# One inference step of a hybrid trunk layer on one core: the samples' page loop, the mixer's sample part and the last down projection in another order

## What is computed

```python
# samples: 1024 past rows in 8 pages of 128, blocks of 32 rows compressed by a two-layer net
ck = rms_norm(compress_block(cmp_rows[:, :, :, 0], phi_k_w1, phi_k_w2), k_cmp_g)   # gelu between the layers
cv = compress_block(cmp_rows[:, :, :, 1], phi_v_w1, phi_v_w2)
s_s = einsum(q, k_selected) ; s_w = einsum(q, k_window)            # scores against the paged and the window keys
# recurrent mixer, one step for each sample and head (4 heads of 128)
S = exp(g)[..., None] * S + k v^T ; o = q S ; o = rms_norm(o, hg_norm_g) * silu(gate)
# feed-forward: 2816 hidden channels in 22 tiles of 128
x = x + (silu(conv(xn2 @ w_gate)) * (xn2 @ w_up)) @ w_down
```

## Time and profile before

| | |
|---|---|
| median of 3 runs | 2120.39 us (2115.72 to 2124.99) |
| the profiled execution | 2122.58 us |
| its span, first to last instruction | 2120.8 us |
| PE busy | 1991.6 us (94%) |
| DVE, ACT, POOL busy | 879.7, 588.8, 155.1 us |
| mean granted clock of PE | 0.953 of full |
| bytes moved by DMA | 148.17 MB |

### The profile page before, as it was taken

How to read it: one execution, slowest core, us unless ns; L and a number is a source line. 1 busy time by engine, 2 the same in 40 slices (tenths; PEclk the granted TensorE clock), 3 DMA queues, 4 the chain that set the end, 5 groups by cost and what they waited for, 6 DMA issues and landing times. The chain is left out here.

```text
span 2120.8 us, 38332 instructions
## 1 busy us (share of the span) xinstructions
PE 1991.6 (94%) x15620; PEld 1771.9 (84%) x15620; DVE 879.7 (41%) x1690; ACT 588.8 (28%) x1192; POOL 155.1 (7%) x214
## 2 busy tenths in 40 slices
PE   5889979999988699897999999999999999999997
PEld 4668656565664688887999999999999999999997
DVE  6223025565612267732223334544334424442453
ACT  5123136555512224413212222211112211111121
POOL 4000001000030033410000000000000000000000
PEclk8899959999999799978999999999999999999999
DMA  8421553000054511213222123111111111111112
GB/s 236 64 69 62 218 128 113 2 2 1 2 171 178 164 32 33 53 42 88 75 75 57 40 63 87 54 49 41 48 52 47 40 49 50 49 38 52 50 30 92
DMA packets 164842, 148.17 MB, mean 70 GB/s; under 512 B 7745, under 2 KB 152082, under 8 KB 163650
## 3 DMA queue, kind: packets, MB, share of 16 engines
q1 hardware_dynamic: 153636, 124.82, 19.7%
q0 software_dynamic: 6208, 17.67, 3.4%
q10 hardware_dynamic: 4864, 3.79, 0.7%
HBM read 120.54 MB, written 29.99 MB: 71 GB/s over the span
## 5 line engine op out<-in xcount | busy, mean ns | idle before, releaser
L247 PE MATMUL psum<-xgl,t_wh 128*128 128x344 f32 x1056 | 338.5, 321 | 0.0
L246 PE MATMUL psum<-xgh,t_wh 128*128 128x344 f32 x1056 | 338.3, 320 | 0.0
L248 PE MATMUL psum<-xgh,t_wl 128*128 128x344 f32 x1056 | 337.6, 320 | 0.0
L247 PEld LDWEIGHTS psum<-xgl,t_wh 128*128 128x128 f32 x1056 | 198.7, 188 | 0.1
L248 PEld LDWEIGHTS psum<-xgh,t_wl 128*128 128x128 f32 x1056 | 198.5, 188 | 0.0
L246 PEld LDWEIGHTS psum<-xgh,t_wh 128*128 128x128 f32 x1056 | 198.3, 188 | 0.1
L248 PE MATMUL psum<-hh,t_wl 128*128 128x344 f32 x528 | 169.2, 320 | 0.0
L246 PE MATMUL psum<-hh,t_wh 128*128 128x344 f32 x528 | 169.1, 320 | 0.0
L247 PE MATMUL psum<-hl,t_wh 128*128 128x344 f32 x528 | 169.0, 320 | 0.0
L466 ACT ACTIVATE t_wh<-t_raw 128x1024 fp32r<-128x1024 f32 x75 | 79.1, 1055 | 205.9 <-PE psum L248 205.9
L518 DVE TENSOR_TENSOR t_wl<-t_raw,t_wh 128x1024 fp32r<-128x1024 f32 x100 | 122.0, 1220 | 34.3 <-ACT t_wh L466 29.2
(11 more groups left out here) (430 smaller groups left out, 3867.9 us busy)
## 6 DMA issues: line engine op xcount, KB each, us to landing
t_raw<-in_w_gate SPq DMA_DIRECT2D x22, 512.0 KB, 3.8
t_raw<-in_w_up SPq DMA_DIRECT2D x22, 512.0 KB, 3.9
t_raw<-in_w_down SPq DMA_DIRECT2D x24, 384.0 KB, 3.4
cmp_pages<-in_cache_kv SPq DMA_DIRECT2D x64, 128.0 KB, 2.2
t_raw<-in_w_in SPq DMA_DIRECT2D x16, 512.0 KB, 4.2
raw_n<-in_w_in SPq DMA_DIRECT2D x24, 256.0 KB, 3.9
r_raw<-in_w_in SPq DMA_DIRECT2D x12, 512.0 KB, 4.4
xh_copy<-xh SPq DMA_DIRECT2D x1, 4128.0 KB, 12.7
```

Source lines behind the costliest of these rows:

```text
L246: pe.matmul(out, wh, xh, start=(first and k == 0), stop=False)
L247: pe.matmul(out, wh, xl, start=False, stop=False)
L248: mm = pe.matmul(out, wl, xh, start=False, stop=(last and k == n - 1))
```

## The change

It has three parts.

1. Page loop: all 128 compression steps come first. Then 24 turns of four transposes (3 for each sample) alternate between banks 7 and 3, and between ACT (even turns) and DVE (odd turns) as the engine that copies them out. The second product stands behind turn 2, the norm's product behind turn 6; scores stand behind every sixth turn as before. `t` and `sq` move to the place of `cmp_pages`, the window loads for samples 2 to 7 to SP's queue, and the reload of `xh` and `xl` now waits for the finished compressed keys.
2. Mixer: keys and values of the four heads lie in four groups of 32 rows, padded with zeros (`k8c`, `v8`). One transpose turns all keys; one POOL operation masks all values, in slot 10; two outer products for two heads each; in the read the queries (one column, repeated 32 times) are stationary and the state's 128 columns move, so each sample's result fills a quarter of 32 rows; ACT and DVE copy it out and two turns of four transposes bring it back to columns.
3. Tail: the last group's `w_down` is split into high and low parts once and kept (`dh`, `dl`), and its product runs over three ranges of columns (0 to 384, 768, 1032), all 8 channels in each. Between channels of the first range stand the transposes of the gate tail, between those of the second and third the transposes of x2 for the tokens of the range before; `store_y` is gone as a block.

Core of the diff, page loop:

```diff
+    bank = lambda q: 3 if q % 2 else 7
+
+    def evacuate(engine, op, q, done):
+
+        s, x = divmod(q, 3)
+        engine.wait_ge(S["tp"], q + 1)
+        if s >= 2:
+            engine.wait_ge(S["sc"], s // 2)
+        to = kwt[:, s % 2, :] if x == 2 else kst[:, s % 2, x * 512:(x + 1) * 512]
+        op(to, c.psum[:, bank(q), :]).then_inc(done, 1)
...
-            sp.wait_ge(S["p1"], 2)
+            for s in range(2, NS):
+                sp.wait_ge(S["tp"], 3 * (s - 2) + 3)
+                sp.dma_start(kwin[:, s % 2, :, :], kw_v[s, :, :, 0:P]).then_inc(w_in[s % 2], 16)
+            sp.wait_ge(S["ck"], 1)
             sp.dma_start(c.xh[:, :, :].bitcast(F32).rearrange("p k t -> p (k t)"), c.xh_dram).then_inc(S["xback"], 16)
             sp.dma_start(c.xl[:, :, :].bitcast(F32).rearrange("p k t -> p (k t)"), c.xl_dram).then_inc(S["xback"], 16)
...
+            def turn(q):
+                s, x = divmod(q, 3)
+                if x == 0:
+                    pe.wait_ge(sel_sp[s], 4 * 16)
+                    pe.wait_ge(sel_pool[s], 4 * 16)
+                if x == 2:
+                    pe.wait_ge(w_in[s % 2], 16 * (s // 2 + 1))
+                if q >= 2:
+                    pe.wait_ge(S["ev"] if q % 2 else S["ea"], q // 2)
+                if q == 1:
+                    pe.wait_ge(S["h"], 2)
                 for p in range(4):
-                    mm = pe.transpose(c.psum[:, TB, p * P:(p + 1) * P], sel[:, s * 8 + 4 * half + p, 0:P], c.ident[:, :])
+                    at = kwin[:, s % 2, p, :] if x == 2 else sel[:, s * 8 + 4 * x + p, 0:P]
+                    mm = pe.transpose(c.psum[:, bank(q), p * P:(p + 1) * P], at, c.ident[:, :])
                 mm.then_inc(S["tp"], 1)
 
...
             order = [(kv, d) for d in range(HD) for kv in range(2)]
-            compress(0, 80)
-            for s in range(NS):
-                x = 80 + 6 * s
-                turn(s, 0)
-                compress(x, x + 2)
-                turn(s, 1)
-                compress(x + 2, x + 4)
-                turn_window(s)
-                compress(x + 4, x + 6)
-                if s % 2:
-                    score(s - 1)
-            pe.wait_ge(S["h"], 2)
-            for g in range(GROUPS):
-                mm = pe.matmul(c.psum[g * HD:(g + 1) * HD, 0, 0:NB], c.w2[0:HD, 0, 0:HD], h[0:HD, g, :], start=True, stop=True)
-            mm.then_inc(S["p2"], 1)
...
+            compress(0, 2 * HD)
+            for q in range(3 * NS):
+                turn(q)
+                if q == 2:
+                    pe.wait_ge(S["h"], 2)
+                    for g in range(GROUPS):
+                        mm = pe.matmul(c.psum[g * HD:(g + 1) * HD, 0, 0:NB], c.w2[0:HD, 0, 0:HD], h[0:HD, g, :], start=True, stop=True)
+                    mm.then_inc(S["p2"], 1)
+                    for s in range(NS):
+                        for g in range(GROUPS):
+                            at = (s % 4) * P + g * HD
+                            mm = pe.matmul(c.psum[0:32, 1 + s // 4, at:at + HD], h[HD:P, g, s * 32:(s + 1) * 32], c.w2[HD:P, 1, HD:P],
+                                           start=True, stop=True)
+                    mm.then_inc(S["p2"], 1)
+                if q == 6:
+                    pe.wait_ge(S["sq"], 1)
+                    pe.matmul(c.psum[:, 0, NB:2 * NB], c.halves[:, :], sq[:, :], start=True, stop=True).then_inc(S["p3"], 1)
+                if q % 6 == 5:
+                    score(q // 3 - 1)
             for b in (5, 6):
                 pe.matmul(c.psum[:, b, :], c.tabrep[:, :], c.one_s[:, 0:512], start=False, stop=True)
```

Mixer (PE, then POOL):

```diff
+                pe.transpose(c.psum[:, X, 0:P], k8c[:, :, :].rearrange("p h s -> p (h s)"), c.ident[:, :]).then_inc(k8_t, 1)
+
+            def sample_outer(h0):
+                if h0 == 0:
+                    pe.wait_ge(k8_done, 1)
+                    pe.wait_ge(vm_done, 1)
                     pe.wait_ge(at_done, 7 * NH)
                     pe.wait_ge(coarse_done, NH)
-                if h >= 2:
-                    pe.wait_ge(new_state, NS * (h - 1))
+                else:
+                    pe.wait_ge(new_state, NS * h0)
                 for j in range(2):
-                    mm = pe.matmul(c.psum[:, X + 2 * ((h + 1) % 2) + j, :], k8[:, h * P:(h + 1) * P], vm[h % 2][:, j * 512:(j + 1) * 512],
-                                   start=True, stop=True)
-                mm.then_inc(outer, 1)
-
-            def sample_read(h):
-                pe.wait_ge(new_state, NS * (h + 1))
-                if h == 0:
+                    for h in (h0, h0 + 1):
+                        r32 = slice(32 * h, 32 * h + 32)
+                        mm = pe.matmul(c.psum[:, X + 2 * ((h + 1) % 2) + j, :], k8[r32, :], vm[r32, j * 512:(j + 1) * 512],
+                                       start=True, stop=True)
+                        if j:
+                            mm.then_inc(outer, 1)
+
+            def sample_read(h0):
+                pe.wait_ge(new_state, NS * (h0 + 2))
+                if h0 == 0:
                     pe.wait_ge(logged, NH)
-                for s in range(NS):
-                    mm = pe.matmul(c.psum[:, O, h * NS + s:h * NS + s + 1], ss[h][:, s * P:(s + 1) * P], q8[:, h, s:s + 1], start=True, stop=True)
+                for h in (h0, h0 + 1):
+                    for s in range(NS):
+                        g0 = 32 * (s % 4)
+                        at0 = (2 * (h % 2) + s // 4) * P
+                        mm = pe.matmul(c.psum[g0:g0 + 32, O + h0 // 2, at0:at0 + P], q8[:, h, s:s + 1].to_broadcast([P, 32]),
+                                       ss[h][:, s * P:(s + 1) * P], start=True, stop=True)
                 mm.then_inc(read, 1)
+
+            def turn_read(half):
+                pe.wait_ge(read_v if half else read_a, 1)
+                for x in range(4):
+                    mm = pe.transpose(c.psum[:, X + half, x * P:(x + 1) * P], sq[:, half * 512 + x * P:half * 512 + (x + 1) * P], c.ident[:, :])
+                mm.then_inc(read_t, 1)
...
-            def masked_values(h):
-                if h == 0:
-                    pool.wait_ge(v_in, 16 * NTT)
-                if h == 1:
-                    pool.wait_ge(y_done, 3 * NH)
-                if h >= 2:
-                    pool.wait_ge(outer, h - 1)
-                pool.tensor_tensor(vm[h % 2].rearrange("p (s x) -> p s x", s=NS),
-                                   v[0:NS, 8, h * P:(h + 1) * P].unsqueeze(1).to_broadcast([NS, NS, P]),
-                                   c.ident[0:NS, 0:NS].unsqueeze(2).to_broadcast([NS, NS, P]), ALU.mult).then_inc(vm_done, 1)
+            def masked_values():
+                pool.wait_ge(v8_in, 16 * NH)
+                pool.wait_ge(m_in, 32)
+                pool.tensor_tensor(vm[:, :].rearrange("p (s x) -> p s x", s=NS), v8[:, :].unsqueeze(1).to_broadcast([P, NS, P]),
+                                   fine[:, 0, 0:NS].unsqueeze(2).to_broadcast([P, NS, P]), ALU.mult).then_inc(vm_done, 1)
```

Tail (PE; the transposes `turn_tail` and `turn_y` are four each):

```diff
+            for r, (a, b) in enumerate(RANGES):
+                for ch in range(KD):
+                    n = KD * r + ch
+                    if r == 0:
+                        pe.wait_ge(raw_free, UL + ch + 3)
+                    if n >= 4:
+                        pe.wait_ge(dn_free, n - 3)
+                    else:
+                        pe.wait_ge(bank_free[0], UL // 2 - BASE + 1)
+                        pe.wait_ge(bank_free[1], UL // 2 - BASE + 1)
+                    for k in range(NL):
+                        if n == 0:
+                            pe.wait_ge(h_ready, KF - NL + k + 1)
+                        mm = three_pass(pe, c.psum[:, n % 4, 0:b - a],
+                                        [(last(wh, dh, ch)[:, k, :], last(wl, dl, ch)[:, k, :], hh[:, k, a:b], hl[:, k, a:b])],
+                                        first=(k == 0), last=(k == NL - 1))
+                    mm.then_inc(dn, 1)
+                    if r == 0 and ch >= 2:
+                        turn_tail(ch - 2)
+                    if r and ch >= 2:
+                        if ch == 2:
+                            pe.wait_ge(dn_free, KD * r)
+                        turn_y(turns[r - 1][(ch - 2) // 2], ch % 2)
+            pe.wait_ge(dn_free, 3 * KD)
+            for tt in turns[2]:
+                turn_y(tt, 0)
+                turn_y(tt, 1)
+
```

360 lines of the change are left out of this document (189 added, 171 removed).

## The result

The changed kernel takes **2094.2 us** (median; 2091.14 to 2098.41), against 2120.35 us for the kernel before, now of four runs: a ratio of 0.9878, with a 95% interval of 0.985 to 0.9906. It is 26.2 us faster, and the forecast was 2095.

The account below looks back on a forecast made before the run. TensorE, busy 94% of the span, was taken as the bound, in its own order, stands and half clock. Page loop 0.9, mixer 19.7 and tail 4.9 gave 25.5 us: 2097.1 profiled, 2095 as median; range 2088 to 2104 at 0.76.

Parts of the forecast that it names:

- The group of 7.8: Page loop: six turns of transposes over two banks and a score take 7.8 us; four such groups 31.2.
- the first group of 10.8: Page loop: the first group is longer by 3.0 us, for the GELUs, the second product and ScalarE's own copies.
- the second of 9.8: Page loop: the second group is longer by 2.0 us, as VectorE's 1.75 us reciprocal sits ahead of the tenth turn.
- the table product and barrier of 2.1: Page loop: the table product and the barrier add 2.1 us to the loop's sum of 52.1.
- the third rival: Tail: the new 2.6 us stand drops the clock and alternating turns keep it down; 2140 us; chance 0.03.
- the fourth rival: Mixer: the outer-product pairs run serially; 2099 us, inside the forecast range, with no chance of its own.
- I take the clock down at T as before, and up again after about 4.5 us: Mixer: half clock from the first read (T, 923.3 us), then full; first read to last projection 20.6 us against 36.5.
- the upper bound (22 for the mixer): Mixer: the gain is 22 us, not 19.7, if the clock never falls.
- The first rival: Mixer: narrow reads and transposes keep the clock at 1.2 GHz to the last projection; 2107 us; chance 0.10.
- 0.55 each with the switch: Tail: each transpose turn added between down matmuls costs 0.55 us, half of the 1.04 row; 9.7 us in all.
- The stand of 2.6: Tail: TensorE waits 2.6 us in the first channel for the last hidden tile's low part.
- Transposes that lose the clock (the second): Page loop: it falls to 1.2 GHz with only transposes and scores left; price 22 us, 2117; chance 0.07.

Follow-up runs that it names:

- e2: The changed kernel with the page loop of the kernel before: 2091.98 us, ratio 0.9866.
- m1: The changed kernel with the old one-column sample reads, two heads together in slots 51 and 54: 2098.84 us, ratio 0.992.
- m2: The changed kernel with the old one-column sample reads, two heads together in slots 53 and 54, where TensorE does not stand: 2096.1 us, ratio 0.9895.
- p1: The changed kernel with the norm's chain moved beside the second score (reciprocal ahead of turn 13, not 9): 2088.22 us, ratio 0.9858.
- p2: p1 plus score products that wait only for their own copies, and four banks instead of two from the seventh turn: 2083.72 us, ratio 0.984.

## Why the prediction was right, point by point

**The total** was right to a microsecond, 2095 against 2094.2, and that closeness is luck. For the profiled execution 25.5 us were forecast and 28.8 measured: the mixer gave 2.3 more than forecast, the tail 2.9 more, and 1.7 went at 877 us. The medians differ by 26.2 because the profiled execution of the kernel before lay 2.2 above its median and that of the changed kernel 0.6 below.

**Page loop.** Forecast 52.1 us, a gain of 0.9; measured 51.2 (three profiles) or 52.7 to 54.1 (five, the first 52.9). The group of 7.8 is 7.67, the first group of 10.8 is 10.65, the second of 9.8 is 9.3 without the fall, the table product and barrier of 2.1 are 2.3. What I didn't have is the clock's fall behind the stand of 1.60 us, though I had the stand. The gain of 0.9 was the right size for a loop without the fall, where it was 1.8, and was 0.1 in the profile taken. I had treated such a fall in the third rival, for a stand of 2.6 us, and not here.

**Outer products.** Forecast 3.8 for pairs that run at once, measured 4.2; the fourth rival (serial pairs) is out.

**The reads.** The step that failed is "I take the clock down at T as before, and up again after about 4.5 us". The clock stayed up, and the stretch took 18.4 us instead of 20.6. I had named the upper bound (22 for the mixer) and taken the lower value, because the old trace shows the fall right behind the stand. That reading was right and one profile was too little for it: the fall at T came in two of ten profiles with the stand. In e2, where it came with the new reads, it went as forecast, back up within 4 us and 19.93 us for the stretch against 20.6. What I had not seen is that the old reads lower the clock by themselves (m1, m2) and so held it down for 30 us. The first rival (clock down to the end, as narrow reads interrupt) had this cause half right and did not come, since the new reads are not of that form.

**What else was named beside the mixer** (copies hidden, one masked product, loads on SP's queue) cost nothing that the rows show: the last projection to the next stage's first takes 16.55 us against 16.44.

**Tail.** Forecast 4.9, measured 7.8. "0.55 each with the switch" is the term that was mis-sized: at 0.43 to 0.45 a turn of four (a channel with one against a channel without), seventeen and one of two come to some 7.7 us and not 9.7. I had halved the row of eight transposes, 1.04 us, which runs from the first start to the last end; in the stream the last transpose's own end lies beside the next matmul. The stand of 2.6 was 1.96. With the 0.3 that I had taken off for switches, these two make the difference of 2.9. The end, 8.3 us behind the last down matmul by the forecast, was 8.30.

**The rivals.** Transposes that lose the clock (the second): not for the loop, as the third and fourth group ran at 0.99 and 1.00; the short fall in the second stands behind a stand, and went with it in p1. The slower case (the third), a stand that drops the clock for the down phase: the stand was there, in two pieces, and the phase took 50.96 to 51.00 us in every profile with this tail, so the clock did not fall.

**What the forecast had no term for** is the 1.7 us at 877 us. It comes with every new loop, 200 us after it, and with no old one. Why is open: the stand ahead of it is the same 1.8 us in all of them, p1 and p2 changed when the loop ends by up to 9 us and it stayed, and I have not found what differs in between. That the loop brings it is a tie seen in fourteen profiles, not a mechanism.
